# A 4-sublayer decoder trunk on one core: turning the W1 and conv-input results with VectorE 32x32 transposes and transfers instead of TensorE transposes

## The reference, cut to what matters

```
h = x * (1 + scale(c)) + shift(c)
x = LayerNorm(alpha * x + (1 + gate(c)) * sublayer(h))
```

```
def short_conv_mixer(h, w_in, conv_w, conv_b, w_out):
    bcu = h @ w_in                                # 2048 -> 3 x 2048
    b_gate, c_gate, u = jnp.split(bcu, 3, axis=-1)
    gated = c_gate * u
    y = conv(gated, conv_w, width 3, causal, one filter per feature) + conv_b
    return (b_gate * y) @ w_out

def sq_relu_mlp(h, w1, b1, w2, b2):
    return jnp.square(jax.nn.relu(h @ w1 + b1)) @ w2 + b2
```

## Time and the profile before

| | |
|---|---|
| median of 3 runs | 2266.32 us |
| lowest, highest | 2265.54, 2266.53 us |
| span of the profiled execution, first to last instruction | 2263.0 us |
| TensorE busy, share of the span | 2228.7 us, 98% |
| VectorE busy | 1686.1 us, 75% |
| ScalarE busy | 1180.4 us, 52% |
| chain that ended last: TensorE, VectorE | 93%, 4% |
| data moved by DMA | 627.09 MB, 277 GB/s |

### The profile page before, as it was taken

The page is one execution under the profiler, slowest core; times in us unless marked ns, Lnnn a source line. Parts: engine busy times, 40 slices in busy tenths (PEclk is TensorE's granted clock), DMA queues, the critical chain, the costliest instruction groups (busy, mean ns, idle before and its releaser), DMA issues.

```text
span 2263.0 us, 28130 instructions
## 1 busy us (share of the span) xinstructions
PE 2228.7 (98%) x10886; PEld 1880.6 (83%) x10886; DVE 1686.1 (75%) x1690; ACT 1180.4 (52%) x1517; POOL 7.7 (0%) x25
## 2 busy tenths in 40 slices
PE   6999999999999999999999999999999999999998
PEld 5999987888888888888888888888888888888886
DVE  7899999986777777778778788878665555555567
ACT  4777784565355345445464444437634544543642
POOL 0000000000000000000000000000000000000000
PEclk9999999999999999999999999999999999999999
DMA  9999998799888888888859778876877667666662
GB/s 353 388 387 397 398 365 310 242 331 326 300 292 277 289 298 284 284 309 273 270 180 371 268 279 306 308 230 218 287 234 235 225 226 241 212 188 189 192 223 103
DMA packets 281525, 627.09 MB, mean 277 GB/s; under 512 B 19233, under 2 KB 27953, under 8 KB 279345
## 3 DMA queue, kind: packets, MB, share of 16 engines
q1 hardware_dynamic: 278432, 608.25, 78.4%
q10 hardware_dynamic: 2960, 17.05, 1.9%
HBM read 623.12 MB, written 2.10 MB: 276 GB/s over the span
## 4 chain that ended last, share of the span: by engine, by line
PE 93%; DVE 4%; issue 1%; DMA 1%; ACT 1%; SPq 0%; DVEq 0%; ACTq 0%
PE bank L1300 27%; PE bank L1302 27%; PE bank L1301 27%; PE bank L1290 3%; PE bank L1293 3%; PE bank L1292 3%; PE bank L1310 2%; DVE mod_acc L910 1%; PE bank L1328 1%; DMA raw<-in_attn_w_qkv 0%; DVE w_low L954 0%; DMA res<-in_x 0%; PE bank L1347 0%; PE bank L1372 0%; PE bank L1360 0%
## 5 line engine op out<-in xcount | busy, mean ns | idle before, releaser
L628 ACT ACTIVATE w_high<-raw 128x1024 fp32r<-128x1024 f32 x752 | 791.4, 1058 | 971.3 <-PE bank L1302 946.2
L954 DVE TENSOR_TENSOR w_low<-raw,w_high 128x1024 fp32r<-128x1024 f32 x752 | 915.8, 1223 | 501.7 <-ACT w_high L628 500.8
L1300 PE MATMUL bank<-w_high,h_high 128*128 128x512 f32 x1632 | 640.1, 392 | 2.9 <-DVE w_low L954 2.9
L1302 PE MATMUL bank<-w_high,h_low 128*128 128x512 f32 x1632 | 635.4, 389 | 0.0
L1301 PE MATMUL bank<-w_low,h_high 128*128 128x512 f32 x1632 | 635.3, 389 | 0.0
L910 DVE SCALAR_TENSOR_TENSOR mod_acc<-mod_raw,cond,mod_acc 128x1024 f32<-128x1024 f32 x345 | 442.1, 1281 | 27.2 <-DMA mod_raw<-in_mod_w 22.8
L1300 PE MATMUL bank<-w_high,hid_high 128*128 128x512 f32 x1120 | 437.2, 390 | 0.0
L1302 PE MATMUL bank<-w_high,hid_low 128*128 128x512 f32 x1120 | 435.8, 389 | 0.0
L1301 PE MATMUL bank<-w_low,hid_high 128*128 128x512 f32 x1120 | 435.8, 389 | 0.0
L1300 PEld LDWEIGHTS bank<-w_high,h_high 128*128 128x128 f32 x1632 | 306.5, 188 | 66.7 <-issue 3.6
L1302 PEld LDWEIGHTS bank<-w_high,h_low 128*128 128x128 f32 x1632 | 306.3, 188 | 64.2
(11 more groups left out here) (151 smaller groups left out, 1165.7 us busy)
## 6 DMA issues: line engine op xcount, KB each, us to landing
raw<-in_mlp_w SPq DMA_DIRECT2D x512, 512.0 KB, 4.5
mod_raw<-in_mod_w SPq DMA_DIRECT2D x368, 512.0 KB, 6.8
raw<-in_attn_w_qkv SPq DMA_DIRECT2D x96, 512.0 KB, 10.6
raw<-in_conv_w_in SPq DMA_DIRECT2D x96, 512.0 KB, 5.5
raw<-in_attn_w_o SPq DMA_DIRECT2D x32, 512.0 KB, 7.2
raw<-in_conv_w_out SPq DMA_DIRECT2D x32, 512.0 KB, 4.7
mod_raw<-in_mod_w SPq DMA_DIRECT2D x32, 256.0 KB, 6.6
gate_row<-in_mod_b ACTq DMA_DIRECT2D x4, 1024.0 KB, 7.5
```

The lines of the kernel that those rows point to most:

```text
L628: act.activation(chunk_slots(n)[0], raw[:, n % NCH], ACT.Copy).then_inc(high_done, 1)
L954: dve.tensor_tensor(low_, raw[:, n % NCH], high.bitcast(F32), ALU.subtract).then_inc(raw_used, 1)
L1300: pe.matmul(dst, high[:, k, c], wh, start=first, stop=False, skip_group_check=True)
L1302: return pe.matmul(dst, low[:, k, c], wh, start=False, stop=last, skip_group_check=True)
```

## The change

The results are turned without TensorE. Behind the split of chunk 3 of the next group VectorE waits for the group's last chunk and transposes each of the two banks in 32x32 blocks into the first half of `stage`, reading the bank at a column stride of four (`turn_quads`). That frees the banks. A 32x32 transposition moves data only inside a quarter of 32 partitions; four transfers from `stage` to `stage`, issued by SP, each from one quarter of 32 partitions to all 128 (128 KB, runs of 1 KB at the destination), finish the turn (`swap_quads`). The features come out in an order of tokens by quarters, and `feat` is read through `by_quads` and `feat_of` to put them back. In SP's order the four transfers stand behind the load of chunk 3 of the group after the next (whose wait is the split in front of the transposes) and wait for the banks to be freed and for `feat` to be free. ScalarE's `late` piece waits for the transfers and moves from chunk 4 to chunk 5, VectorE's from chunk 5 to chunk 6. `copy_rows`, `empty` and `turn` go. Relu reads and writes `feat`; the product of units 4 to 7 is made in four instructions instead of one.

```diff
+            def swap_quads(u):
+
+                i = u - U_CIN
+                if 0 < i <= NG:
+                    sp_.wait_ge(y_copied, i)
+                else:
+                    sp_.wait_ge(post_done, CREDIT_STAGE + (u if i <= 0 else u - NG))
+                sp_.wait_ge(banks_free, UNIT_GROUPS[u] + BANK0 + CREDIT_BANKS + 1)
+                for a in range(QUADS):
+                    sp_.dma_start(feat_quads[:, a, :], turned_quads[32 * a:32 * (a + 1)]).then_inc(swapped, 16)
+
+            swap_at = {(w + 1) * NCH + SLOTS - 1 + NCH: u for u, w in enumerate(UNIT_GROUPS)}
             for n in range(N_HEADS + 2 * AHEAD, N_CHUNKS):
                 load_chunk(n)
+                if n in swap_at:
+                    swap_quads(swap_at[n])
                 load_tiles(TILE_AT[n - AHEAD], TILE_AT[n - AHEAD + 1])
...
                 for j in range(first, NCH):
                     high(w * NCH + j)
-                    if late and j == SLOTS:
+                    if late and j == SLOTS + 1:
                         late()
...
             def turned_hidden(layer, f, g):
-                w = f * (2 * NG) + g + W_MLP[layer]
-                act.wait_ge(rows_turned, f * NG + U_MLP[layer] + g + 1)
-                act.wait_ge(post_done, f * NG + CREDIT_STAGE + S_MLP[layer] + g)
+                act.wait_ge(swapped, SWAP_DMAS * (f * NG + U_MLP[layer] + g + 1))
                 b1 = V_B1 + layer * (FF // P)
                 for m in range(GT):
                     at = f * KT + g * GT + b1 + m
-                    ins = act.activation(feat[:, m, :], bank[2 * (g % 2) + m // 2][:, T * (m % 2):T * (m % 2 + 1)],
-                                         ACT.Relu, bias=vec[:, at:at + 1])
-                ins.then_inc(banks_free, 1)
-                act.wait_ge(banks_free, w + BANK0 + CREDIT_BANKS + 1)
-                act.activation(feat, feat, ACT.Square).then_inc(squared, 1)
+                    ins = act.activation(feat_of(m), feat_of(m), ACT.Relu, bias=vec[:, at:at + 1])
+                ins.then_inc(lifted, 1)
+                act.wait_ge(lifted, f * NG + g + layer * NG * FC + 1)
+                act.activation(stage[:, 1], stage[:, 1], ACT.Square).then_inc(squared, 1)
                 act.wait_ge(squared, f * NG + g + layer * NG * FC + 1)
...
-                act.activation(hid_high[:, g * GT:(g + 1) * GT, :], feat, ACT.Copy).then_inc(hidden_high, 1)
+                act.activation(by_quads(hid_high[:, g * GT:(g + 1) * GT, :]), feat, ACT.Copy).then_inc(hidden_high, 1)
...
+            def turn_quads(u):
+
+                w = UNIT_GROUPS[u]
+                if u:
+                    dve.wait_ge(swapped, SWAP_DMAS * u)
+                dve.wait_ge(chunk_mult, w * NCH + CREDIT_SPLIT + NCH)
+                for t in range(TT):
+                    ins = dve.transpose(turned_quads.rearrange("p c (m t s) -> p t m c s", m=GT, t=TT)[:, t],
+                                        bank[2 * (u % 2) + t][:, :].rearrange("p (m s c) -> p m c s", m=GT, c=QUADS))
+                ins.then_inc(banks_free, 1)
...
-                steps(f * (2 * NG) + g + W_MLP[layer], None, late, SLOTS + 1, each, SLOTS if f or g else NCH)
+                steps(f * (2 * NG) + g + W_MLP[layer], None, late, SLOTS + 2, each, SLOTS if f or g else NCH)
+                turn_quads(U_MLP[layer] + f * NG + g)
...
-                dve.wait_ge(banks_free, w + BANK0 + CREDIT_BANKS + 1)
+                dve.wait_ge(swapped, SWAP_DMAS * (U_CIN + i + 1))
...
-                dve.tensor_tensor(gated[:, :, 2:T + 2], feat, y[:, g * GT:(g + 1) * GT, :], ALU.mult
-                                  ).then_inc(conv_step, 1)
+                    dve.wait_ge(y_copied, NG)
+                for m in range(GT):
+                    ins = dve.tensor_tensor(gated[:, m, 2:T + 2].rearrange("p (t a s) -> p t a s", t=TT, a=QUADS),
+                                            feat[:, m * TT:(m + 1) * TT],
+                                            y[:, g * GT + m, :].rearrange("p (t a s) -> p t a s", t=TT, a=QUADS),
+                                            ALU.mult)
+                ins.then_inc(conv_step, 1)
...
-            def turn(u, par, rows):
-
-                pe.wait_ge(rows_done, u + 1)
-                for m in range(GT):
-                    for t in range(TT):
-                        at = T * (m % 2) + P * t
-                        ins = pe.transpose(bank[2 * par + m // 2][:, at:at + P], rows[:, t, m * P:(m + 1) * P],
-                                           ident[:])
-                ins.then_inc(rows_turned, 1)
```

More of the change, by code:

```diff
@@ L72, in build_trunk @@
     U_CIN = NG * FC
-    TURN_AFTER = 0
+    UNIT_GROUPS = ([W_MLP[0] + f * 2 * NG + g for f in range(FC) for g in range(NG)]
+                   + [W_CIN + i for i in range(3 * NG)]
+                   + [W_MLP[1] + f * 2 * NG + g for f in range(FC) for g in range(NG)])
+    QUADS = P // 32
+    SWAP_DMAS = 16 * QUADS
     QUARTERS = KT // GT
@@ L319, in build_trunk @@
         post_done = sem("post_done")
-        rows_done = sem("rows_done")
         half_mult = sem("half_mult")
-        rows_turned = sem("rows_turned")
+        swapped = sem("swapped")
+        y_copied = sem("y_copied")
+        lifted = sem("lifted")
         pads = sem("pads")
@@ L712, in _ @@
                     load_gate(0)
[L714 to L722, removed]
             def output_high(o):
@@ L843, in turned_conv @@
             def turned_conv(i):
[L844 to L850, removed]
+                act.wait_ge(swapped, SWAP_DMAS * (U_CIN + i + 1))
+                act.activation(by_quads(y[:, i * GT:(i + 1) * GT, :]), feat, ACT.Copy).then_inc(y_copied, 1)
             for i in range(3 * NG):
-                highs(W_CIN + i, (lambda: turned_conv(i - 1)) if i else None, SLOTS if i else NCH)
-                copy_rows(i % 2, rows_loop)
+                highs(W_CIN + i, (lambda: turned_conv(i - 1)) if 0 < i <= NG else None, SLOTS if i else NCH)
                 if i < NG:
                     load_later(1, i)
-            tail(2, lambda: turned_conv(3 * NG - 1))
+            tail(2)
             mlp(1)
@@ L1101, in tail @@
                 for g in range(NG - 1):
-                    steps(w0 + g, None, (lambda: take_both(n, g - 1)) if g else before, SLOTS if g else SLOTS + 1)
+                    steps(w0 + g, None, (lambda: take_both(n, g - 1)) if g else before, SLOTS if g else SLOTS + 2)
                 last = (w0 + NG - 1) * NCH
@@ L1138, in _ @@
             tail(0)
+            def turn_quads(u):
[7 more added lines that the diff above has]
+                ins.then_inc(banks_free, 1)
             def turned_hidden(layer, f, g):
                 dve.wait_ge(hidden_high, f * NG + g + layer * NG * FC + 1)
-                dve.tensor_tensor(hid_low[:, g * GT:(g + 1) * GT, :], feat,
-                                  hid_high[:, g * GT:(g + 1) * GT, :].bitcast(F32), ALU.subtract
+                high = hid_high[:, g * GT:(g + 1) * GT, :].bitcast(F32)
+                dve.tensor_tensor(by_quads(hid_low[:, g * GT:(g + 1) * GT, :]), feat, by_quads(high), ALU.subtract
                                   ).then_inc(post_done, 1)
@@ L1229, in _ @@
             for i in range(3 * NG):
-                steps(W_CIN + i, None, (lambda: turned_conv(i - 1)) if i else None, SLOTS + 1,
+                steps(W_CIN + i, None, (lambda: turned_conv(i - 1)) if i else None, SLOTS + 2,
                       (lambda k: residual(1, k)) if i == 1 else None, SLOTS if i else NCH)
+                turn_quads(U_CIN + i)
             tail(2, lambda: turned_conv(3 * NG - 1))
@@ L1416, in chunk, with group @@
                 return ins
-            def group(w, par, high, low, ready=None, hook=None, hook_at=TURN_AFTER):
+            def group(w, par, high, low, ready=None):
                 pe.wait_ge(banks_free, w + BANK0 + 1)
@@ L1499, in o_ready_first, with tail @@
                 o_ready(j)
-            def tail(n, high, low, ready, first_ready, before=None):
+            def tail(n, high, low, ready, first_ready):
                 w0 = W_TAIL[n]
                 for g in range(NG - 1):
-                    group(w0 + g, g % 2, high, low, ready if g else first_ready, None if g else before)
+                    group(w0 + g, g % 2, high, low, ready if g else first_ready)
                 last_group(n, (NG - 1) % 2, high, low, ready)
@@ L1510, in mlp @@
             def mlp(layer):
-                w0, s0, u0 = W_MLP[layer], S_MLP[layer], U_MLP[layer]
+                w0, s0 = W_MLP[layer], S_MLP[layer]
                 for f in range(FC):
-                    wf, sf, uf = w0 + f * (2 * NG), s0 + f * NG, u0 + f * NG
+                    wf, sf = w0 + f * (2 * NG), s0 + f * NG
                     for g in range(NG):
                         if f or g:
-                            group(wf + g, g % 2, h_high, h_low, None,
-                                  (lambda: turn(uf + g - 1, (g - 1) % 2, rows_loop)) if g else None)
```

(11 more changed lines are left out.)

24 lines of the change are left out of this document (13 added, 11 removed).

## The result

The changed kernel takes 2335.05 us (median of 4 runs, 2333.34 to 2338.55) where the kernel before takes 2265.99: a ratio of 1.0305, interval 1.0291 to 1.0320. It is 69 us slower; 2245 us had been forecast, with a range to 2268.

A forecast was written before the change was run, and what follows sets the result against it. The prediction took TensorE to bound nearly every stage from 470 to 2190 us. Its terms, -39.2 + 6 + 5 + 2 + 5 = -21 us, gave a 2242 us span, 2245 us timed, range 2227 less a microsecond to 2268.

The forecast's parts named there:

- What leaves TensorE: Turns of eight transposes on TensorE, 0.89 us each over 44 units: 39.2 us, the whole possible gain.
- The transposes: VectorE's two transposes of a 128x512 bank per unit: 1.35 us taken, between 1.3 and 2.6 us.
- The landing: Time from turned to transfers landed, per unit: 4.2 us in quiet stages, 5 in MLP 0's middle stages, 5.5 in the crowded one.
- t0: The end of a group's last matmul; chunk j of the next group is due at t0 + 2.72 j.
- The deadlines of t0+10.3 and t0+9.2: Latest landing without a stall: t0+10.3 for chunk 6's split, t0+9.2 for the hidden piece in a block's first W2 group.
- Terms (2) to (4): Stalls: (2) first block of MLP 0, +6 us; (3) MLP 0's 12 other units, +5; (4) MLP 1's 16 units, +2.
- Term (5): Conv units 4 to 7: VectorE's work overdraws four groups by about 3 us net; +5 us, the conv's first units included.
- The rival of late landings: Behind the split of chunk 5 in every MLP group, ScalarE's wait for transfers becomes the bound; slower, 2290 us; chance 0.2.
- Everything hidden: Transfers land in 3.1 us, every quiet-stage landing before t0+8, about 4 us of stalls left: 2231 us; chance 0.2.
- nearly all given back, by VectorE: VectorE becomes the bound in groups at 470, 493 and 1284 to 1470 us: about 2264 us, or 2256; chance 0.15.

The follow-up runs named there:

- the short ones above: Waits made in the kernel before: TensorE stopped 30 times in MLP 1 by six small GpSimd writes each, 1.7 us a wait; 2328.11 us, ratio 1.0268.

## Why the prediction was wrong

*What leaves TensorE: right.* The run without transfers is 29.6 us faster than before with 6.8 us of waits left (spare slots counted), which fits 39.2 us: in the profiled executions the span is 28.6 us shorter, with 5.8 us more of waits and about 4.5 us less of clock than before, 38.9 us together.

*The transposes: right.* 1.31 us a pair against 1.35 taken; the column stride of four costs nothing. The slowdown of non-contiguous reads that the Trainium skill (SBUF — State Buffer, section "Door 1: The DMA port swizzle") tells of for matmuls is not seen in VectorE's read here: 0.69 us a bank against the 0.68 of the earlier trace rows.

*The landing: the step that failed.* "Turned at t0+3.7, with a tile t0+4.9" and "I take 4.2 us ... 5 us ... 5.5 us" were both too small; from the transposes to ScalarE's start it took 6.3 us on average, over the 36 units that ScalarE takes from the transfers. In the 13 MLP groups with a wait over 2 us (t0 is 16.3 us before the wait) the transposes end at t0+5.9 on average (3.7 to 9.4), since VectorE is often late by more than one tile, and ScalarE starts 7.1 us later, at t0+12.0 to 14.4. The deadlines of t0+10.3 and t0+9.2 were right, and 13.0 less 10.3 is 2.7 us of wait by itself. The working took the issue from a load (0.37 us, 0.60 measured), the latency from an idle tail, and a median for the queue, where a deadline is missed by the cases above the median.

*The sizes that followed.* Terms (2) to (4), +6, +5 and +2, measured 18 us in the first block (five waits from 488 to 573 us), 27 us in the rest of MLP 0, 18 us in MLP 1. Term (5) was 5 us, from an overdraft of "about 3 us net" that the four rows give as 2.2; the conv input has 8.3 us, of which 5 us are in its first groups, where the residual is added, and not in units 4 to 7 alone.

*The rival of late landings was right in kind*: with landings 2 us later it gave 63 us of stalls and 2290 us. The stalls are 72.4 us, 71.4 more than before. What it lacked, and the whole prediction with it, is the clock: "its clock is already at the upper level" was said of what the change removes and never asked of the waits it brings. The sum of the profiled executions: -39.2 (turns) + 71.4 (waits) + 40.7 (slower matmuls, from TensorE's busy time) = +72.9, of +73.8 us between the spans. Of the 40.7 us the mean clock accounts for 35; each of the waits costs a little beyond its length too, as the short ones above did, and the two parts were not separated further. The medians are only 69 us apart, since the profiled execution after was the slowest of its four. Every execution with both numbers on record takes about 1.8 us more than its span; of the 3.3 us that the prediction added, the other 1.5 are the spread of the runs.

*Everything hidden* falls by the first window after, with TensorE idle for 12 us; *nearly all given back, by VectorE*, falls by the run without transfers.

## What to carry to other kernels

A hop through a transfer is to be set against a deadline with its slowest case in the stage where it runs, and what stands behind the waiting instruction in its queue is to be moved in front of it. Start the hop with the first instruction that can run: two transposes moved in front of one split, with their transfers one load earlier, were worth 57 us. Where TensorE is the bound, price a wait of a few us by the clock it loses too: here 5.0 us for 3.3.

## What was not expected of the hardware

A transfer from SBUF to SBUF of 128 KB is issued in 0.60 us, one of 512 KB from HBM in 0.37. On ScalarE's own queue such a transfer landed later, 5.3 against 3.2 us. A 3.3 us wait of TensorE cost 5.0 us, two of 1.7 us 4.1. Four times fewer issues of the same bytes brought the data only 0.4 us sooner.
